# Fine levels of a gated scan as 32x32 blocks, and the next scan's first work ahead of the readout

## The reference

```python
# S_t = diag(exp(g_t)) S_{t-1} + k_t v_t^T,   o_t = S_t^T q_t
b = jnp.cumsum(gc, axis=2)
S_new = jnp.exp(b_last[:, :, 0, :])[..., None] * S + jnp.einsum('bhck,bhcv->bhkv', k_dec, vc)
o_inter = jnp.einsum('bhck,bhkv->bhcv', qc * jnp.exp(b), S)
a = jnp.einsum('bhtk,bhsk,bhtsk->bhts', qc, kc, jnp.exp(diff))
...
ox_f, _ = chunk_scan(qx, kxf, gxf, vx, sc_f, True)
ox_b, _ = chunk_scan(flip(qx), flip(kxb), flip(gxb), flip(vx), sc_b, True)
```

## Time and profile before

| | us |
|---|---|
| median of 3 runs | 2534.23 (2530.31 to 2535.01) |
| the profiled execution | 2532.31 |
| its span | 2530.5 |
| PE busy | 2331.3 (92%) |
| DVE busy | 971.4 (38%) |
| ACT busy | 823.4 (33%) |
| POOL busy | 61.7 (2%) |
| chain that ended last | PE 72%, DMA 12%, ACT 8%, DVE 5% |

### The profile page before, as it was taken

How to read it: one execution, slowest core, us unless ns; L and a number is a source line. 1 busy time by engine, 2 the same in 40 slices (tenths; PEclk the granted TensorE clock), 3 DMA queues, 4 the chain that set the end, 5 groups by cost and what they waited for, 6 DMA issues and landing times.

```text
span 2530.5 us, 33013 instructions
## 1 busy us (share of the span) xinstructions
PE 2331.3 (92%) x13502; PEld 1542.1 (61%) x13502; DVE 971.4 (38%) x1586; ACT 823.4 (33%) x1253; POOL 61.7 (2%) x34
## 2 busy tenths in 40 slices
PE   6989889999999977779999889999999999999997
PEld 4944777786888977679989778333333333333332
DVE  5466443443252386666654655311111111111112
ACT  4367432332242445635535663111111111111101
POOL 0000000000000014300000000000000000000000
PEclk8999999999999998889999999999999999999999
DMA  9287054432231400225546246999999999999995
GB/s 344 68 299 231 3 177 140 133 100 88 71 125 54 147 1 1 100 67 168 199 179 206 99 107 235 390 424 428 429 428 428 428 428 429 428 428 428 428 429 248
DMA packets 142518, 603.76 MB, mean 239 GB/s; under 512 B 6752, under 2 KB 52064, under 8 KB 117696
## 3 DMA queue, kind: packets, MB, share of 16 engines
q1 hardware_dynamic: 142400, 602.11, 60.8%
HBM read 601.03 MB, written 1.05 MB: 238 GB/s over the span
## 4 chain that ended last, share of the span: by engine, by line
PE 72%; DMA 12%; ACT 8%; DVE 5%; issue 1%; SPq 1%; ACTq 0%; DVEq 0%
PE bank L1024 71%; DMA last_e<-in_b_up 11%; DMA ring<-in_ada_w 1%; ACT arena L1943 1%; ACT arena L2312 1%; ACT modp L1718 1%; PE bank L1249 0%; ACT w_high L2152 0%; ACT arena L2221 0%; ACT wide_p L2209 0%; ACT w_split L1784 0%; PE bank L1621 0%; DVE arena L2782 0%; DVE last_sums L2721 0%; DMA ring<-in_ffn_w_up 0%
## 5 line engine op out<-in xcount | busy, mean ns | idle before, releaser
L1024 PE MATMUL bank<-arena 128*64 128x512 f32 (+6 forms) x2392 | 472.3, 502 | 77.2 <-ACTq L784 29.1
L1024 PEld LDWEIGHTS bank<-arena 128*64 128x64 f32 (+2 forms) x2392 | 199.8, 162 | 308.1 <-issue 194.8
L1024 PE MATMUL bank<-hT_high,w_split 128*128 128x512 f32 (+1 forms) x1408 | 346.6, 337 | 2.4 <-DVE hT_low L2383 2.4
L1024 PE MATMUL bank<-ring,arena 128*64 128x512 f32 (+1 forms) x1248 | 301.4, 598 | 20.6 <-ACT arena L2312 11.8
L1024 PEld LDWEIGHTS bank<-hT_high,w_split 128*128 128x128 f32 x1408 | 242.1, 190 | 31.4 <-issue 2.8
L1024 PE MATMUL bank<-hT_low,w_split 128*128 128x512 f32 (+1 forms) x704 | 236.6, 336 | 0.0
L3059 DVE TENSOR_SCALAR arena<-bank 128x512 f32<-128x512 f32 x32 | 22.1, 692 | 551.5 <-PE bank L1024 551.3
L1024 PEld LDWEIGHTS bank<-ring,arena 128*64 128x64 f32 (+1 forms) x1248 | 99.7, 142 | 207.2 <-issue 181.2
L1024 PE MATMUL bank<-freed_w,arena 128*64 128x512 f32 x768 | 170.6, 595 | 8.1 <-ACT arena L2312 5.5
L1024 PEld LDWEIGHTS bank<-hT_low,w_split 128*128 128x128 f32 x704 | 133.6, 190 | 14.4 <-issue 1.0
L1024 PEld LDWEIGHTS bank<-freed_w,arena 128*64 128x64 f32 x768 | 53.3, 137 | 118.3 <-issue 103.0
(11 more groups left out here) (424 smaller groups left out, 4068.1 us busy)
## 6 DMA issues: line engine op xcount, KB each, us to landing
ring<-in_ada_w SPq DMA_DIRECT2D x24, 2048.0 KB, 8.1
ring<-in_w_gate SPq DMA_DIRECT2D x24, 2048.0 KB, 25.3
arena<-in_w_up SPq DMA_DIRECT2D x24, 2048.0 KB, 26.2
ring<-in_w_down SPq DMA_DIRECT2D x24, 2048.0 KB, 29.8
arena<-in_w_down SPq DMA_DIRECT2D x24, 2048.0 KB, 29.6
ring<-in_w_up SPq DMA_DIRECT2D x24, 2048.0 KB, 26.8
arena<-in_w_gate SPq DMA_DIRECT2D x24, 2048.0 KB, 24.6
ring<-in_ffn_w_up SPq DMA_DIRECT2D x44, 1024.0 KB, 7.7
```

The source lines that it names most:

```text
L1024: return pe.matmul(o, l, r, start=start, stop=stop)
```

## The change

- The diagonal and levels 2 to 6 (h up to 16) lie in blocks of 32 tokens. They are now made as 32x32 products, one for each of the 8 blocks of 32 tokens and 4 heads: 32 small products where there were 8 of 128x128. The output's partition quarter `z` goes through the four quarters, j through tile and head. All of a level lies in 256 columns of one bank.
- DVE keeps such a level with one instruction of 128x256 in a small buffer `rFs[b]`, where there were two of 128x512. When a scan has ended, four copies (`keep_diagonals`, two on ACT for z = 0, 1 and two on DVE for z = 2, 3) put the 32x32 diagonals into the 128x128 blocks.
- There are two buffers of blocks, `rAs[0]` (the old `rA`) and `rAs[1]` (over `rope` and a new 512 columns behind it), and POOL clears the scan's own with a memset ahead of its D(0). For scan 1 the memset waits until s(7) of scan 0 is done, for scans 2 and 3 for the readout of two scans before, and for scan 0 for the projections' last group. ACT's copies of levels 0 and 1 wait for it in place of the diagonal.
- PE's order: level -1 and level 0 of the next scan stand ahead of the readout of the scan before. ACT takes the readout behind level 0, DVE adds it after s(1). In scan 3, `head_squares` stands ahead of x(2) and x(3), where it stood ahead of x(1) and x(2), and writes to a part of the arena.
- The readout waits for the four copies in place of level 6's. The masks are 128x320 for 128x1792, with a small `ident32` made once by a reduction.

```diff
+        rAs = [region(15360, 2, 4, P), nc.alloc_sbuf_tensor_at("second_blocks", [P, 2, 4, P], F32, offset=rope_at)]
+        rFs = [region(19968, 2 * 4, GROUP32), region(20224, 2 * 4, GROUP32)]
...
+            for scan, (d, b) in enumerate(SCANS):
+                if scan == 1:
+                    pool.wait_ge(qk_scaled, NL + 1)
+                elif scan:
+                    pool.wait_ge(psum_ready, group["ro", *SCANS[scan - 2], 1] + 1)
+                pool.memset(rAs[scan % 2][:, :, :, :], 0.0).then_inc(coarse_zeroed, 1)
                 pool.wait_ge(sums_ready, scan + 1)
...
+                        kx, qx = (rks[d, b], rq[:, 4 * b:4 * b + 4, :]) if n < 0 else (KL[n % 2], QL[n % 2])
+                        for j in range(2 * 4):
+                            for z in range(P // GROUP32):
+                                tok = slice(j // 4 * P + z * GROUP32, j // 4 * P + (z + 1) * GROUP32)
+                                m = mm(ps[z * GROUP32:(z + 1) * GROUP32, j * GROUP32:(j + 1) * GROUP32],
+                                       kx[:, j % 4, tok], qx[:, j % 4, tok], True, True)
...
+            for scan, (d, b) in enumerate(SCANS):
+                await_next(kdec_ready)
+                for n in range(-1, NL + 1):
+                    level(d, b, n)
+                    if n == 0 and scan:
+                        readout(scan - 1, *SCANS[scan - 1])
+                    if 1 <= n <= 4:
+                        context_state(d, b, n - 1)
+                    if 0 <= n < 4:
+                        turn_keys(d, b, n)
+            readout(len(SCANS) - 1, *SCANS[-1])
...
+            def keep_diagonals(d, b):
+
+                act.wait_ge(freed["dve"], nth[group["lev", d, b, NL - 1, 0]])
+                for z in range(2):
+                    cut = slice(z * GROUP32, (z + 1) * GROUP32)
+                    do(act.activation(rAs[b][cut, :, :, cut].rearrange("p t i c -> p (t i) c"), rFs[b][cut, :, :],
+                                      ACT.Copy), diagonals_act)
...
-                            if n in (1, 2):
-                                head_squares(0, n - 1)
+                            if n in (2, 3):
+                                head_squares(0, n - 2)
...
                     def keep(n):
+                        ps = take(("lev", d, b, n, 0))[:, 0:2 * 4 * GROUP32].rearrange("p (j c) -> p j c", c=GROUP32)
+                        if n < 0:
+                            do(TT(rFs[b], ps, ident32[:, :].unsqueeze(1).broadcast_to((P, 2 * 4, GROUP32)), ALU.mult), F)
+                            return
+                        at = (d * len(FINE) + n - 2) * GROUP32
+                        m = masks[:, at:at + GROUP32].unsqueeze(1).broadcast_to((P, 2 * 4, GROUP32))
+                        do(dve.copy_predicated(rFs[b], m, ps), F)
```

More of the change, by code:

```diff
@@ L104, in constants @@
     put("item", np.tile(np.arange(ITEMS + 2, dtype=np.float32), (P, 1)))
[L105 to L109 removed]
+    masks = np.zeros((P, 2, len(FINE), GROUP32), np.float32)
+    s, tt = (p % GROUP32)[:, None], np.arange(GROUP32)[None, :]
+    for n, h in enumerate(FINE):
+        masks[:, 0, n] = (s // (2 * h) == tt // (2 * h)) & (s % (2 * h) < h) & (tt % (2 * h) >= h)
+        masks[:, 1, n] = (s // (2 * h) == tt // (2 * h)) & (s % (2 * h) >= h) & (tt % (2 * h) < h)
     return c, masks.reshape(P, -1)
@@ L574, in program, with tiles, plan_readout @@
         ACT_LEVELS = (0, 1, NL)
-        for d in range(2):
-            for b in range(2):
-                for n in range(-1, NL + 1):
-                    for t in ([0] if n == NL else XS):
-                        add(("lev", d, b, n, t), "act" if n in ACT_LEVELS else "dve")
-                    if 1 <= n <= 4:
-                        add(("st", d, b, n - 1), "act")
-                    if 0 <= n < 4:
-                        add(("kt", d, b, n), "act")
-                for t in XS:
-                    add(("ro", d, b, t), "dve" if d else "act")
+        def tiles(n):
+            return XS if n in (0, 1) else [0]
+        SCANS = [(d, b) for d in range(2) for b in range(2)]
+        def plan_readout(d, b):
+            for t in XS:
+                add(("ro", d, b, t), "dve" if d else "act")
+        for scan, (d, b) in enumerate(SCANS):
+            for n in range(-1, NL + 1):
+                for t in tiles(n):
+                    add(("lev", d, b, n, t), "act" if n in ACT_LEVELS else "dve")
+                if n == 0 and scan:
+                    plan_readout(*SCANS[scan - 1])
+                if 1 <= n <= 4:
+                    add(("st", d, b, n - 1), "act")
+                if 0 <= n < 4:
+                    add(("kt", d, b, n), "act")
+        plan_readout(*SCANS[-1])
         for h in range(2):
@@ L922, in _ @@
             pool.wait_ge(psum_ready, group[unit_end[HG_UNITS[-1]]] + 1)
-            for scan, (d, b) in enumerate((d, b) for d in range(2) for b in range(2)):
+            for scan, (d, b) in enumerate(SCANS):
[4 more added lines that the diff above has]
+                pool.memset(rAs[scan % 2][:, :, :, :], 0.0).then_inc(coarse_zeroed, 1)
                 pool.wait_ge(sums_ready, scan + 1)
@@ new lines, in readout @@
+            def readout(scan, d, b):
+                late = 1 - d
+                pe.wait_ge(last_scaled, 2 * d + b + 1)
+                pe.wait_ge(diagonals_act, 2 * (scan + 1))
+                pe.wait_ge(diagonals_dve, 2 * (scan + 1))
+                pe.wait_ge(freed["act"], nth[group["lev", d, b, NL, 0]])
+                for t in XS:
+                    key = ("ro", d, b, t)
+                    ps = bank(key)
+                    for i in range(4):
+                        h = 4 * b + i
+                        o = ps[:, i * P:(i + 1) * P]
+                        mm(o, last_q[:, i, t * P:(t + 1) * P], rS[:, i, :], True, False)
+                        if t == late:
+                            mm(o, rC[:, i, :], rv[:, 1 - late, h * P:(h + 1) * P], False, False)
+                        m = mm(o, rAs[scan % 2][:, t, i, :], rv[:, t, h * P:(h + 1) * P], False, True)
+                    close(m, key)
@@ L2103, in _ @@
                             take_level(d, b, n - 1)
+                        if n == 1 and ended and ended[0] == 0:
+                            take_readout(*ended)
                         if 2 <= n <= 5:
```

98 lines of the change are left out of this document (37 added, 61 removed).

## The result

Beside the kernel before, the changed kernel took 2537.91 us (median of 7; before 2533.44 of 7): ratio 1.0022, 95% interval 1.0013 to 1.0032. Measured a second time it gave 1.0009 [1.0000, 1.0019]. The kernel before against itself gave 1.0009 [0.9999, 1.0018], so that a loss of 0.1 to 0.2% is at the edge of what can be told; that the 6 to 7 us of gain are not there is clear. Forecast was 2527.4. The profiled execution of after is the slowest of its seven, 2544.46 us (span 2542.6, before 2530.5).

What follows compares the result with a forecast made beforehand. In the scans no engine is full; the chain through PE, DVE, ACT and POOL decides. Gains inside scans and at two boundaries, less losses at 0-1 and the end, sum to -6.8 us: 2527.4, 8 in 10 from 2518 to 2545.

Steps and rivals of the forecast that it cites:

- L(3) gives 0.75 of the 0.92 back: Inside scans 1 and 2: shorter level 3 on PE cuts ACT's 0.92 us wait, so x(5), s(5) come 0.75 earlier.
- The price of a level: PE's fine level of 64 records of 32 columns: taken as 1.0 us, 0.75 less than before.
- The keep is one instruction of 128x256 ... so 1.1 saved; `last_q` ends at 13.7. Now s(6) waits for x(6): DVE inside scans 1 and 2: keep takes 0.40 us, saving 1.1, so s(6) starts 1.1 us earlier, at 14.5.
- rival 4: POOL's memset and D(0) hold s(6) and the keep, levels 3, 4 no shorter: 5.4 us less gain, 2532.8; chance 0.15.
- I let it come at 4.5: Boundaries: PE's full clock returns 4.5 us after s(7)'s end; at 1-2 half clock then costs 0.7 us.
- rival 1: Half clock lasts until the readouts end: price 18.3 us, 2546, slower; chance 0.15, whole or in good part.
- Boundaries 1-2 and 2-3: From s(7)'s end to the next x(2): 11.1 and 12.6 us forecast, gains of 1.0 and 1.2.
- two copies of 32x256 at 0.35: DVE's diagonal copies at boundaries 1-2 and 2-3: 0.35 us each, s(0) done at 2.8, hidden by PE.
- Boundary 0-1: POOL's memset and D(0) wait for s(7), so PE stands: x(2) at 16.0 us for 12.28, loss 3.7.
- Scan 3 "+0.2": Scan 3 on ACT: `head_squares` adds 1.74 us, the wait of 1.62 is gone, 0.1 hand-over stays: 0.2 lost.
- the start "-0.6": Scan 0's start: only level -1 is shorter, 0.6 us gained; the memset lies under DVE's last scans.
- The end: Scan 3's end: readout waits for ACT's two copies (0.8 us) and has more half clock (0.7): 1.5 lost.

Runs made afterwards that it cites:

- extra products: Changed kernel plus 128x128 products on PE that nobody reads, while it waits ahead of levels 0 and 2 to 7: 2531.94 us, ratio 0.9988.
- the hidden readout: Changed kernel, early memset, readout behind next scan's level 1 and turned keys 1, diagonal copies behind s(0): 2532.80 us; with weights' transfer released earlier 2525.38.
- the early memset: Changed kernel, but scan 1's memset waits for scan 0's first scale only, not its last: ratio 1.0013.
- once PE was off the chain at the boundary and the weights' transfer with it: Readout behind next scan's level 1 and turned keys 1, weights' transfer released by scan 2's level 7: narrow levels 2525.68 us, full blocks 2529.77.

## Why the prediction was wrong, step by step

- *"L(3) gives 0.75 of the 0.92 back"*: right at full clock. In scan 0 s(5) ends at 11.65 us counted from x(2), 11.75 forecast. In scan 1 level 4's records take 2.24 us for 1.40, and s(5) ends at 12.34: 0.16 gained on before's 12.50. The price of a level, 1.0 us, was too high by a quarter at full clock and about right at half clock. The Trainium skill's floor of some 25 ns from start to start (TensorE: Matmul & The Clock Gate, "Wait — 56ns, not 53.3ns?") would make 1.6 us of it, an estimate. The trace does not agree for records that go through the four quarters: 64 in 0.76 us, 12 ns each.
- *"The keep is one instruction of 128x256 ... so 1.1 saved; `last_q` ends at 13.7. Now s(6) waits for x(6)"*: this step failed in scans 1 and 2. I took `last_q` at its length of before, 1.48 us, and not by its end. POOL's D(7), memset and D(0) hold both instructions, and s(6)'s end has not moved (5.38 us behind s(5) in both). It is rival 4's mechanism in its first half, D(0) and the memset standing for the old D(0). I had also taken the 2.28 us of s(6) and the 2.89 of D(0) as lengths, where each held a wait for the other engine. Only the keep behind s(6) gave its 1.0 us. Of the 1.6 us missing in each of two scans 0.6 were lost up to s(5), at half clock, and 1.3 here, with 0.3 more than forecast behind s(6). With POOL idle in scan 0, s(6) fell to 0.69 as said; `last_q` beside D(7) took 2.53 us there too, which is most of the 0.3 us that scan 0 is above the forecast.
- *"I let it come at 4.5"*: failed, the largest term. The levels made short took PE's clock away not only behind level 5: it fell 5.5 us behind x(2), 11 us earlier than before, and full clock came 8.4 us behind s(7) at 1-2. The 1.5 us of the kernel before, from which I had started, belonged to one execution (6.9 in the second). That return is 3.9 us later than assumed, where rival 1 had put its deciding point at 3.6 for each of four readouts. Half clock did not last to the readouts' ends, as rival 1 had it in full, but in good part it came. Boundaries 1-2 and 2-3 are 2.8 and 2.3 us above the forecast, of which the clock, restored by extra products, gives back 2.1 and 1.8 (11.7 for 11.1 forecast, 13.1 for 12.6).
- *"two copies of 32x256 at 0.35"*: right with POOL idle (0.61 for both in scan 3), and the same failure as with `last_q` beside it: 1.97 us for both at 1-2, 2.56 at 0-1. So s(0) ends 3.9 us behind s(7) and not 2.8, and PE stands 0.84 us before level 0. Putting the copies behind s(0) was part of the kernels with the hidden readout and not tried alone.
- *Boundary 0-1*: 16.67 (15.56 in the second profile) for 16.0. The chain was right: memset 0.95 (1.5 assumed), D(0) 1.95, x(0), s(0), level 0 at half clock. Two errors cancel in part: s(0) ends 0.3 us earlier than forecast, and PE behind it loses 0.7 more to half clock. The experiment with the early memset gives 13.8.
- *Scan 3 "+0.2"* and the start "-0.6": 23.5 for 23.3 as said. The start grew by 0.2. POOL's memset is not the reason: it lies under DVE's last scans as said, and x(0) ends at 933.24, 5.6 us before s(0) starts. Level -1 is shorter (1.08 us), but PE, which had stood for 11 us, then does all of level 0 at half clock, 3.79 us; before, full clock came back within levels -1 and 0 (5.19 us for both). The end grew by 1.7, 1.5 forecast.

The differences to the forecast, over the scans of the profiled pair: -6.8, and then +3.2 (insides 1, 2), +2.8 and +2.3 (boundaries 1-2, 2-3), +0.7 (0-1), +0.3 (inside 0), +0.8 (start), +0.2 (end) make +3.5; measured +3.4. The rivals 1 and 4 had been weighed apart, and both came in part, at 0.15 each. What I left out of the range's reasoning is that they are not independent of the main case: the same short levels that save PE's time take away its clock.

## What to carry to other kernels

Taking work from an engine whose clock follows its load must be priced at the clock that it will have after, on what stands behind; here 16 us less of busy PE bought nothing in this order, and 4 us of the kernel's time once PE was off the chain at the boundary and the weights' transfer with it. Where two engines hold each other up, compare the ends of instructions with the other engine's ends; a length read from a trace is no cost that can be carried to another place. Move a step in an order only after looking at everything that it releases: the readout held back x(2), then the turned keys, then a transfer of weights, and each move paid only when the next one was made.

## What the hardware showed that was not expected

- Products of 32 columns on four quarters of the array: 64 in 0.76 us at full clock, 1.08 at half clock, not twice as long.
- The granted clock was 0.50 for 23.9 us in a row with 14.6 us of busy PE in them; in the kernel before its stretch at the same place was 6.8 us long, with 5.3 us busy, and 10.2 us with 8.0 busy in the second profile.
- A DVE product with both inputs in SBUF ended 1.08 to 1.12 us (128x1024) or 0.54 to 0.55 us (128x512) behind the end of POOL's subtraction beside it, in three kernels; copies of 32x256 took 1.0 and 1.3 us each beside POOL and 0.3 with POOL idle.
- The same kernel's scans differ by 2 us between executions, by the clock that single products happen to meet: the readout's first half at 1-2 in the kernel before, level 3 of scans 0 and 1 and the readout at 0-1 in the changed one.
